# Attention outputs in four 32-column strips instead of two 64-column halves, in a fused NSA and MLA layer

## The chip, the cores and the metric

One core of a Trainium2 chip runs the whole kernel as one program. The metric is the device time of one execution in microseconds (us), as the median of several runs. The profile is one execution taken by the hardware profiler.

## The reference, cut to what matters

The reference is one layer of a hybrid decoder: 512 prompt tokens and 8 decode tokens (each with 4096 cached positions) go through Native Sparse Attention (three branches: compressed, selected, sliding window) and Multi-head Latent Attention (MLA), each with 8 heads, then gates, projections, an output projection, a norm and a residual. All arrays are float32. For the prompt the part that matters here is the last product of attention, probabilities times values:

```python
o_s = jnp.einsum('bqgrkl,bqgkld->bqgrd', p_s.astype(v_sel.dtype), v_sel)      # selected branch
o_w = jnp.einsum('bqgrs,bsgd->bqgrd', p_w.astype(kvw.dtype), kvw[..., 1, :])  # sliding window
p = _masked_softmax(s, mask)                                                  # MLA
return jnp.einsum('bhqs,bsc->bqhc', p.astype(c.dtype), c)
```

Each is, for one head and one tile of 128 query tokens, a sum over blocks of 128 keys of (128 keys x 64 value columns), transposed, times (128 keys x 128 queries). The MLA values are expanded per head to 64 columns ahead of the stage (`vm`).

## The kernel before

The program is written engine by engine, with every order and every semaphore by hand; nothing is planned by a compiler. It has four stages: the input projection (to about 130 us), a preparation (to about 200 us), the attention stage (about 200 to 510 us), and the gates, projections and output (to the end).

**The attention stage** works on 96 *units*. A unit is one branch (selected, window or MLA), one head and one tile `tl` of 128 queries; it has `tl + 1` key blocks, 1 to 4. Two units with neighbouring heads are a *pair*; there are 48 pairs. TensorE (PE) runs a loop over steps d = 1 to 49. Its parts, in the order of a step, with the line of their matmuls:

- `scores(d)` (L1132): the scores of the two units of pair d, 64 or 96 rows of weights by 128 columns.
- `dec_transposes(d - 1)` (L1279), where a decode chunk was scored in the step ahead: transposes with 128 columns.
- `dec_scores` (L1210) or `latent_scores` (L1235, with L1239 at the end of every second one): decode scores. Both load weights of 128 rows and 32 columns, four at a time, into the four 32-column strips of the array (`32 * j:32 * j + 32` in the bank). Ten steps have the first, 32 the second (two of these are ahead of the first call of `outputs`: d = 0 and 1).
- `outputs(d - 2)` (L1153): the probabilities of pair d - 2 times values; this is what the change touches. It is called in 48 steps.
- `latent_outputs` (L1250, 128x32 weights, 256 moving columns; twice in each of 16 steps) or `dec_outputs` (L1219, 128x32 weights; in 10 steps), where a decode chunk is due.
- `gate_half` (L1266, 128x128 weights, 260 moving columns), in 16 steps.
- `dec_keys` (L1200) and `transposes` (L1140): 128-column transposes of cached keys and of the probabilities of pair d - 1.

In `outputs(p)` the values are the weights (stationary), the transposed probabilities `PTb[e]` are moving, and both heads of the pair (e = 0, 1) write their half of the partitions of bank 3. Ahead of it PE waits for `pt_by_V` and `pt_by_A`: VectorE (DVE, L2148) and ScalarE (ACT, L1678) copy the transposed probabilities out of PSUM. Behind it, `o_ps` releases DVE, which reads the bank (L2172, L2174), and the two copies.

The softmax of the units runs on DVE (L2140, mask and sum; L1782 and L1783, scaling) and ACT (L1670, exponential). Decode chunks take a chain of their own over DVE (L2192 to L2238), ACT (L1684, L1687, L1484) and back to PE.

**Loads.** SyncE (SP) issues the cached latents (`latents`, L619 to L622), windows (`windows`, L609) and weights in one queue, each behind a wait for a free slot, which PE frees with `mv_ps` or `do_ps`. GpSimd (POOL) gathers rotary keys and selected rows (L710).

A float32 matmul is carried out as two instruction pairs, each a weight load (PEld) and a matmul (PE); the profile counts these.

Of the kernel before, what the change touches and what calls it, by code (L numbers as in the profile page):

```python
# [16 lines left out]
P = 128  # L17
# [146 lines left out]
def build(nc, t):  # L164

    ctx = ExitStack()
    with ctx:
# [35 lines left out]
        bank = [ctx.enter_context(nc.psum_tensor(f"bank{i}", [P, 512], F32)) for i in range(8)]  # L203
# [65 lines left out]
        PTb = [c_(512) for _ in range(2)]  # L269
# [254 lines left out]
        def qbank(i):  # L524
            return bank[(3, 0, 4, 1)[i % 4]]
# [27 lines left out]
        def unit(u):  # L553

            if u < 32:
                return 2, 2 * (u // 8) + u % 2, (u % 8) // 2
            v = u - 32
            return (v % 4) // 2, 2 * (v // 16) + v % 2, (v % 16) // 4
# [4 lines left out]
        def group_of(p):  # L563

            return (p, True, True) if p < 16 else (16 + (p - 16) // 2, p % 2 == 0, p % 2 == 1)

        def pt_by(u):
            return "A" if u % 2 else "V"
# [240 lines left out]
        def _(pe):  # L809
# [156 lines left out]
            for b in range(4):  # L966
                for e in range(2):
                    n = 4 * e + b
                    mm = pe.matmul(bank[5][32 * e:32 * e + 32, 0:P], QZraw[:, n * 64 + 32 * e:n * 64 + 32 * e + 32], KcT[:, n * P:(n + 1) * P],
                                   start=(b == 0), stop=(b == 3))  # L970
# [16 lines left out]
            for n in range(10, 16):  # L987
                c, w = GROUPS[n]
                mm = pe.transpose(bank[7][0:w, P + 8 * n:P + 8 * n + 8], projD[0:DEC, c:c + w], ident8)
# [9 lines left out]
            for k in range(4):  # L999
                mm = pe.matmul(bank[2][32 * k:32 * k + 32, :], kcBD[:, (k // 2) * 32:(k // 2 + 1) * 32], qTraw[:, k * 512:(k + 1) * 512],  # L1000
                               start=True, stop=True)
# [4 lines left out]
            for i, h in enumerate(HQ):  # L1006
# [10 lines left out]
                for j in range(3):  # L1017
                    mm = pe.matmul(qbank(i)[:, :], wq[:, j * 1024 + h * P:j * 1024 + (h + 1) * P],  # L1018
                                   qdnT[:, j * TOK:j * TOK + SEQ], start=(j == 0), stop=(j == 2))
                mm.then_inc(S["qm_ps"], 1)  # L1020
                if i == 1:
                    pe.wait_ge(S["prep_by_act"], BY_ACT["sct"])
                    for tl in range(TILES):
                        mm = pe.transpose(bank[2][:, tl * P:(tl + 1) * P], pcP[:, tl * P:(tl + 1) * P], ident)
# [5 lines left out]
                if i == 4:  # L1030
# [3 lines left out]
                    for j in range(3):  # L1034
                        for s in range(4):
                            mm = pe.matmul(bank[6][32 * s:32 * s + DEC, 0:256], qdnT[:, j * TOK + SEQ:(j + 1) * TOK],
                                           wq[:, j * 1024 + s * 256:j * 1024 + (s + 1) * 256], start=(j == 0), stop=(j == 2))
                    mm.then_inc(S["prep_ps"], 1)
                if i == 6:
                    pe.wait_ge(S["prep_by_act"], BY_ACT["qd8"])  # L1040
                    for h2 in range(8):
                        mm = pe.transpose(bank[6][:, 256 + 8 * h2:264 + 8 * h2], qd8[0:DEC, h2 * P:(h2 + 1) * P], ident8)
# [3 lines left out]
            for p2 in range(4):  # L1046
# [3 lines left out]
                for ck in range(2):  # L1050
                    mm = pe.matmul(bank[KM_BANK[p2]][:, :], wk[:, ck * 512 + p2 * P:ck * 512 + (p2 + 1) * P],
                                   cT[:, ck * TOK:ck * TOK + SEQ], start=(ck == 0), stop=(ck == 1))
# [3 lines left out]
            for b in range(4):  # L1056
                for e in range(2):
                    n = 4 * e + b
                    mm = pe.matmul(bank[5][32 * e:32 * e + 32, 384:512], PcZ[:, n * 64 + 32 * e:n * 64 + 32 * e + 32], VcD[:, n * P:(n + 1) * P],
                                   start=(b == 0), stop=(b == 3))  # L1060
# [5 lines left out]
            for half in range(2):  # L1066
                for j in range(4):
                    h = 4 * half + j
                    c = h * 8 - 24 * half
                    mm = pe.matmul(bank[7][32 * j:32 * j + 32, half * 256:(half + 1) * 256], qmd[0:64, c:c + 32],  # L1070
                                   wkT[0:64, h * 256:(h + 1) * 256], start=True, stop=True)
            mm.then_inc(S["absorbed"], 1)

            for tl in range(TILES):
                if tl == 2:
                    pe.wait_ge(S["qmd"], 3)
                    for blk in range(4):
                        mm = pe.transpose(bank[6][:, blk * P:(blk + 1) * P], Pd[:, blk * P:(blk + 1) * P], ident)
# [6 lines left out]
                for ck in range(2):  # L1085
                    mm = pe.matmul(bank[VM_BANK[tl]][:, :], cT[:, ck * TOK + tl * P:ck * TOK + (tl + 1) * P],
                                   wv[:, ck * 512:(ck + 1) * 512], start=(ck == 0), stop=(ck == 1))
# [4 lines left out]
            for tl in range(TILES):  # L1092
                mm = pe.transpose(bank[4][:, tl * P:(tl + 1) * P], pcP[:, tl * P:(tl + 1) * P], ident)
# [14 lines left out]
            def values(br, tl, kb, h):  # L1108
                if br < 2:
                    at = kb * 256 + br * P + (h // 4) * 64  # L1110
                    return VV[:, at:at + 64]
                return vm[:, kb * 512 + h * 64:kb * 512 + (h + 1) * 64]
# [30 lines left out]
            def outputs(p):  # L1143

                g, first, last = group_of(p)
                for u in (2 * p, 2 * p + 1):
                    pe.wait_ge(S["pt_by_" + pt_by(u)], u // 2 + 1)
                if first and g:
                    pe.wait_ge(S["o"], g)
                br, h, tl = unit(2 * p)  # L1150
                for kb in range(tl + 1):
                    for e in range(2):
                        mm = pe.matmul(bank[3][64 * e:64 * e + 64, 0:P], values(br, tl, kb, h + e), PTb[e][:, kb * P:(kb + 1) * P],  # L1153
                                       start=(first and kb == 0), stop=(last and kb == tl))
                mm.then_inc(S["o_ps"], 1)

# [131 lines left out]
            for d in range(1, PAIRS + 2):  # L1288
# [8 lines left out]
                if d >= 2:  # L1297
                    outputs(d - 2)
# [83 lines left out]
            def quad(bk, k, rhs, first, last):  # L1382

                for j in range(4):
                    mm = pe.matmul(bk[32 * j:32 * j + DEC, 0:P].rearrange("p (r c) -> p r c", r=2), h_[k][:, SEQ:TOK],
                                   rhs.rearrange("p (r j c) -> p r j c", r=2, j=4)[:, :, j], start=first, stop=last)
                return mm
# [40 lines left out]
            for v, (kind, x) in enumerate(tail):  # L1428
# [20 lines left out]
                for hf in range(2):  # L1449
                    bk = bank[2 * (v % 2) + hf]  # L1450
                    bank_free(pe, v, 2 * (v % 2) + hf)
                    if kind in ("ga", "gb", "ma", "mb"):
                        for k in range(KM):
                            at = k * 256 + (x % 2) * P
                            mm = pe.matmul(bk[:, 0:HALF], gate_w[g % 2][:, at:at + P], X2[:, k * TOK + hf * HALF:k * TOK + (hf + 1) * HALF],  # L1455
                                           start=(k == 0), stop=(k == KM - 1))
                    else:
                        for k in range(KM):
# [3 lines left out]
                            if x < TILES:  # L1462
                                mm = pe.matmul(bk[:, :], h_[k][:, x * P:(x + 1) * P], w, start=(k == 0), stop=(k == KM - 1))  # L1463
                            else:
                                mm = quad(bk, k, w, k == 0, k == KM - 1)
# [1178 lines left out]
```

## Time and profile before

| | us |
|---|---|
| runs of the kernel before (3) | 743.08, 744.10, 747.31 |
| median | 744.1 |
| span of the profiled execution | 739.6 |
| PE busy in it | 692.4 (94%), 5305 matmul instructions |
| DVE busy | 440.6 (60%) |
| ACT busy | 211.5 (29%) |
| POOL busy | 123.4 (17%) |

The span runs from the first to the last instruction of the profiled execution; the time of a run includes what lies around it. The engines run beside each other, and a busy share says nothing of what waits for what; the chain of work followed back from the last instruction does. In the lines of the profile L12 is line 12 of the kernel, PE the matmuls, PEld the weight loads, "issue" a time for which nothing that the profile shows was waited for. Matmuls are pipelined and their ends are modelled, so neighbouring groups overlap in the rows; starts are measured.

### The profile page before, as it was taken

Reading aid. Unit: us, or ns where it says so; the run is one execution under the profiler, and the core shown is the slowest. Engines: PE = TensorE matmul, PEld = TensorE weight load, DVE = VectorE, ACT = ScalarE, POOL = GpSimd, SP = SyncE. Lnnn points to the kernel's source line nnn. Section 1 sums busy time; section 2 is a strip of 40 time slices with the busy share of each in tenths; the row PEclk is TensorE's granted clock in tenths of the full one; section 3 lists DMA queues with packets and bytes.
Section 4 is the critical chain, followed back from the end, with each engine's and each line's share of the span. In section 5 each row is a group of like instructions: output and inputs, shape, how many; then the busy total and the mean of one; then the engine's idle time right before and its main releaser. Section 6 shows DMA issues by size and latency. Waiting matters only on the chain.

```text
span 739.6 us, 14391 instructions
## 1 busy us (share of the span) xinstructions
PE 692.4 (94%) x5305; PEld 443.7 (60%) x5305; DVE 440.6 (60%) x1233; ACT 211.5 (29%) x579; POOL 123.4 (17%) x130
## 2 busy tenths in 40 slices
PE   9997999999988979789999999899999999999996
PEld 4443444644555655467675676557778888885452
DVE  3297799478666756764654554542577565644244
ACT  0302215555334434433533442321110101110111
POOL 0343340113042230321412202320000000000000
PEclk9999999999999999999999999999999999999998
DMA  9999994951779999967755686996210303026011
GB/s 343 414 414 421 418 399 159 384 219 49 250 276 336 315 381 343 393 222 277 276 209 185 237 285 232 332 334 259 72 57 1 114 1 114 1 91 280 29 47 41
DMA packets 57367, 170.27 MB, mean 230 GB/s; under 512 B 7537, under 2 KB 7690, under 8 KB 50514
## 3 DMA queue, kind: packets, MB, share of 16 engines
q1 hardware_dynamic: 47352, 120.68, 45.1%
q0 software_dynamic: 9600, 48.38, 16.6%
q8 instruction: 43, 0.70, 0.4%
q10 hardware_dynamic: 346, 0.29, 0.1%
q14 instruction: 26, 0.21, 0.1%
HBM read 164.99 MB, written 8.52 MB: 235 GB/s over the span
## 4 chain that ended last, share of the span: by engine, by line
PE 75%; DMA 9%; DVE 5%; issue 5%; SPq 3%; ACT 2%; another core or an unknown queue 1%; DVEq 0%; ACTq 0%
PE bank L1423 18%; PE bank L855 7%; PE bank L1463 7%; PE bank L1266 7%; DMA W<-w_attn 4%; PE bank L1153 4%; PE bank L1132 3%; PE bank L1250 3%; PE bank L1235 3%; PE bank L1018 3%; PE bank L1140 3%; DMA projP<-x 2%; PE bank L1200 2%; PE bank L1455 2%; DMA ring<-latent 2%
## 5 line engine op out<-in xcount | busy, mean ns | idle before, releaser
L710 POOL DMA_INDIRECT KRR<-krT,idxi x64 | 61.2, 957 | 221.9 <-PE bank L1239 207.1
L855 PE MATMUL bank<-W,XG 128*128 128x494 f32 x192 | 85.2, 589 | 4.2 <-DMA W<-w_attn 3.7
L1484 ACT ACTIVATE projP<-bank 128x128 f32<-128x128 f32 (+5 forms) x87 | 33.9, 391 | 110.0 <-PE bank L1423 47.5
L2438 DVE TENSOR_TENSOR projP<-projP,bank 128x260 f32<-128x260 f32 x83 | 33.9, 422 | 45.1 <-PE bank L1423 44.4
L855 PEld LDWEIGHTS bank<-W,XG 128*128 128x128 f32 x192 | 35.8, 195 | 41.0 <-issue 39.8
L1266 PE MATMUL bank<-W 128*128 128x260 f32 x256 | 60.4, 389 | 0.0
L1484 ACT ACTIVATE W<-bank 128x512 f32<-128x512 f32 (+2 forms) x69 | 40.1, 582 | 69.8 <-PE bank L898 18.7
L1670 ACT ACTIVATE projP<-bank,projP 128x128 f32<-128x128 f32 (+3 forms) x96 | 49.7, 524 | 29.9 <-DVE projP L2140 29.5
L2140 DVE CUSTOM_DVE_ANT_0 bank<-bank,maskb 128x128 f32<-128x128 f32 (+3 forms) x96 | 45.8, 507 | 15.9 <-PE bank L1132 11.2
L1266 PEld LDWEIGHTS bank<-W 128*128 128x128 f32 x256 | 47.3, 190 | 10.4 <-issue 3.3
L1463 PE MATMUL bank<-ring,W 128*128 128x512 f32 x112 | 49.5, 594 | 1.3 <-issue 1.3
L710 POOL DMA_INDIRECT ring<-cmp,idxi x32 | 38.7, 1209 | 72.1 <-DVE VV L1849 52.5
L1132 PE MATMUL bank<-W 64*128 64x128 f32 (+7 forms) x192 | 46.2, 467 | 1.4 <-ACT projP L1670 1.0
L1849 DVE TENSOR_TENSOR VV<-ring 128x1024 f32<-128x1024 f32 x32 | 39.1, 1222 | 7.4 <-DMA ring<-cmp,idxi 5.0
L1140 PE MATMUL bank<-cst,projP 128*128 128x128 f32 x240 | 37.8, 287 | 2.4 <-issue 1.3
L1423 PE MATMUL bank<-ring 128*128 128x260 f32 x168 | 38.3, 383 | 0.7 <-DVE ring L2404 0.7
L1463 PEld LDWEIGHTS bank<-ring,W 128*128 128x128 f32 x112 | 21.1, 190 | 27.7 <-issue 27.5
L1423 PEld LDWEIGHTS bank<-ring 128*128 128x128 f32 x168 | 31.8, 190 | 6.3 <-issue 1.5
L1140 PEld LDWEIGHTS bank<-cst,projP 128*128 128x128 f32 x240 | 28.2, 145 | 11.9 <-issue 6.4
L1423 PE MATMUL bank<-W 128*128 128x260 f32 x144 | 34.7, 384 | 0.4 <-DVE projP L2434 0.4
L1235 PE MATMUL bank<-ring,projP 128*32 128x128 f32 x800 | 29.2, 276 | 5.1 <-issue 3.2
L1744 ACT ACTIVATE projP<-projP 128x260 f32<-128x260 f32 x28 | 11.4, 420 | 72.8 <-DVE projP L2438 72.8
(439 smaller groups left out, 1145.7 us busy)
## 6 DMA issues: line engine op xcount, KB each, us to landing
ring<-latent SPq DMA_DIRECT2D x200, 256.0 KB
XG<-latent SPq DMA_DIRECT2D x56, 256.0 KB
W<-w_gate SPq DMA_DIRECT2D x12, 1024.0 KB, 4.7
W<-w_attn SPq DMA_DIRECT2D x16, 494.0 KB, 9.8
ring<-w_out SPq DMA_DIRECT2D x2, 2048.0 KB
o_win<-win SPq DMA_DIRECT2D x1, 4088.0 KB
W<-xT SPq DMA_DIRECT2D x1, 2080.0 KB, 11.2
projP<-x SPq DMA_DIRECT2D x1, 2048.0 KB
```

The source lines that it names most:

```text
L710: pool.indirect_dma_start(out=dst, out_offset=None, in_=src, in_offset=bass.IndirectOffsetOnAxis(ap=idxi[:, col:col + 1], axis=0)).then_in ...
L855: mm = pe.matmul(bank[2 * (u % 2) + n][:, 0:GW], XG[:, k * TOK + tl * P:k * TOK + (tl + 1) * P], w_part(half, k, n), start=(k == 0), stop= ...
L1132: pe.matmul(bank[x % 2][:, 0:width], q, kk, start=True, stop=True).then_inc(S["s"], 1)
L1140: mm = pe.transpose(pt_bank(u)[:, kb * P:(kb + 1) * P], Pb[u % 4][:, kb * P:(kb + 1) * P], ident)
L1235: pe.matmul(bank[5][32 * j:32 * j + 32, 0:P], latent_q(b, ck, 2 * i2 + q2), page(m, j, q2, 256 + ck * P, 256 + (ck + 1) * P), start=(i2 == ...
L1266: mm = pe.matmul(bank[6][:, 0:HALF], gate_w[g % 2][:, at:at + P], X2[:, k * TOK + hf * HALF:k * TOK + (hf + 1) * HALF], start=(k == 0), st ...
L1423: mm = pe.matmul(pair_bank(v, name)[:, 0:HALF], stationary(a, kk), moving(b, kk), start=(kk == 0), stop=(kk == inner - 1))
L1463: mm = pe.matmul(bk[:, :], h_[k][:, x * P:(x + 1) * P], w, start=(k == 0), stop=(k == KM - 1))
L1484: return act.activation(dst, src, ACT.Copy, scale=scale)
L1670: act.activation(Pb[u % 4][:, 0:w], bank[u % 2][:, 0:w], ACT.Exp, bias=NMp[:, u:u + 1], scale=-1.0, accum_out=RSp[:, u:u + 1]).then_inc(S[ ...
L1849: dve.tensor_tensor(sum4, x[:, 0:1024], x[:, 1024:2048], ALU.add).then_inc(S["summed"], 1)
L2140: dve.tensor_tensor_reduce(bank[u % 2][:, 0:w], bank[u % 2][:, 0:w], maskb[:, 512 - w:512], -1.0, 1e38, ALU.add, ALU.min, NMp[:, u:u + 1]) ...
```

## The change

The block of `outputs` no longer does one matmul for each head with 64 weight columns, but two for each head with 32. The loop runs over four strips: strip 0 and 1 are the lower and upper 32 value columns of head e = 0, strip 2 and 3 those of e = 1. Each writes its 32 partitions of bank 3. Both strips of a head have the same moving operand. What is computed, the bank, the place of `outputs` in the step, the waits ahead of it and the semaphore behind it are as they were. No other line changes.

```diff
                 br, h, tl = unit(2 * p)
                 for kb in range(tl + 1):
-                    for e in range(2):
-                        mm = pe.matmul(bank[3][64 * e:64 * e + 64, 0:P], values(br, tl, kb, h + e), PTb[e][:, kb * P:(kb + 1) * P],
+                    for strip in range(4):
+                        e, lo = strip // 2, 32 * (strip % 2)
+                        mm = pe.matmul(bank[3][32 * strip:32 * strip + 32, 0:P], values(br, tl, kb, h + e)[:, lo:lo + 32], PTb[e][:, kb * P:(kb + 1) * P],
                                        start=(first and kb == 0), stop=(last and kb == tl))
                 mm.then_inc(S["o_ps"], 1)
```

## Rows read from the trace of the kernel before

**Rows 1.** The page's first part: busy us, share of the span, instructions.
```profile
PE 692.4 (94%) x5305; PEld 443.7 (60%) x5305; DVE 440.6 (60%) x1233; ACT 211.5 (29%) x579; POOL 123.4 (17%) x130
```

**Rows 2.** The page's fourth part: the chain that ended last, by engine and line.
```profile
PE 75%; DMA 9%; DVE 5%; issue 5%; SPq 3%; ACT 2%; another core or an unknown queue 1%; DVEq 0%; ACTq 0%
...
by line: PE bank L1423 17.6%; PE bank L855 7.5%; PE bank L1463 7.5%; PE bank L1266 7.0%; issue 4.6%; DMA W<-w_attn 4.1%; PE bank L1153 3.8%; PE bank L1132 3.5%; PE bank L1250 3.5%; PE bank L1235 3.4%; PE bank L1018 3.1%; PE bank L1140 2.7%;
```

**Rows 3.** Windows of the attention stage: stretch, length, busy, clock, DMA share, GB/s.
```profile
200.00:300.00 100.00, 88.17 (x1259) 58.36 (x1259) 65.61 (x247) 40.89 (x139) 26.72 (x28) 0.98 0.94 333
300.00:515.00 215.00, 197.30 (x2237) 136.62 (x2235) 112.92 (x395) 75.17 (x231) 45.79 (x48) 0.98 0.75 268
```

**Rows 4.** Groups of L1153 by form; then those that start before 300 us.
```profile
L1153 PE MATMUL bank<-projP,VV 128*64 128x128 f32 x320 | 25.5, 286 | 4.0 <-issue 2.1 <-DVE projP L2148 2.0
L1153 PE MATMUL bank<-projP,W 128*64 128x128 f32 x160 | 12.3, 282 | 1.3 <-DVE projP L2148 1.0 <-issue 0.3
...
L1153 PE MATMUL bank<-projP,VV x24: 272/273/323, 285.1 to 297.6; 128*64 128x128 f32 x24
```

**Rows 5.** Timeline of PE, in three steps: start us, us, line, shape, instructions.
```profile
382.70 1.08 PE L1235 MATMUL bank<-XG,projP 128*32 128x128 f32 x32
383.60 0.40 PE L1239 MATMUL bank<-KRR,OB 128*32 128x128 f32 x8
383.93 1.09 PE L1153 MATMUL bank<-projP,VV 128*64 128x128 f32 x16
384.95 1.53 PE L1200 MATMUL bank<-cst,ring 128*128 128x128 f32 x12
...
402.78 0.44 PE L1153 MATMUL bank<-projP,VV 128*64 128x128 f32 x4
403.15 0.65 PE L1219 MATMUL bank<-ring,W 128*32 128x64 f32 x32
403.74 3.77 PE L1266 MATMUL bank<-W 128*128 128x260 f32 x16
...
409.10 1.08 PE L1235 MATMUL bank<-ring,projP 128*32 128x128 f32 x32
410.11 0.44 PE L1153 MATMUL bank<-projP,VV 128*64 128x128 f32 x4
```

**Rows 6.** Timeline of PE at the start of the stage.
```profile
202.13 0.62 PE L1178 MATMUL bank<-projP,cst 8*32 8x128 f32 x16
202.67 1.13 PE L1132 MATMUL bank<-W 96*128 96x256 f32 x4
```

**Rows 7.** The chain of waits in order of time, around the first window load.
```profile
265.21 8.83 DMA ring<-win
```

**Rows 8.** Timeline of PE in a step with keys; in brackets the idle time ahead.
```profile
390.89 0.45 PE L1279 MATMUL bank<-cst,W 128*128 128x128 f32 x1 [1.52 <-ACT W L1484]
```

**Rows 9.** The five largest waits of PE, 200 to 515 us: total us, times, longest.
```profile
PE bank L1250 <- issue: 4.3, 5, 1.7
PE bank L1235 <- issue: 3.2, 6, 1.2
PE bank L1153 <- DVE projP L2148: 3.0, 4, 1.1
PE bank L1279 <- ACT W L1484: 2.9, 4, 1.5
PE bank L1153 <- issue: 2.4, 4, 1.2
```

**Rows 10.** Timeline of PE at a hitch.
```profile
464.88 0.43 PE L1153 MATMUL bank<-projP,VV 128*64 128x128 f32 x2
465.69 0.27 PE L1153 MATMUL bank<-projP,VV 128*64 128x128 f32 x1 [0.38 <-issue]
466.42 0.27 PE L1153 MATMUL bank<-projP,VV 128*64 128x128 f32 x1 [0.46 <-issue]
467.13 0.69 PE L1250 MATMUL bank<-ring,projP 128*32 128x256 f32 x8 [0.45 <-issue]
```

## Prediction

> **What bounds the kernel now.** I read the page's busy table first [rows 1]: TensorE (PE) is busy 94% of the 739.6 us span, the next engine (VectorE, DVE) 60%. A busy PE is not yet the bound, so the chain of work that ended last came second [rows 2]: 75% of it is PE, 9% DMA, 5% DVE. Third, the stages [rows 3]. The changed line, L1153, runs only in the attention stage (206 to 509 us). From 200 to 300 us PE is busy 88.2 of 100 us and the DMA engines 94%; from 300 to 515 us PE is busy 197.3 of 215 us and DMA 75%. The change can therefore be worth most where PE ends the chain, and less in the first 100 us, where the transfers are nearly full. L1153 is 3.8% of the chain [rows 2], 28.1 us, of its 25.5 + 12.3 = 37.8 us busy [rows 4]: 74% of this line's time lies on the path that sets the end.
>
> Fourth, what a group of small matmuls costs on PE, from the timeline of PE in single steps. The time from one group's start to the next group's start is what counts, as the ends are modelled. A float32 matmul is two instructions, so a block of L1153 (two heads, e = 0 and 1) is 4 instructions. L1153 with 4 instructions takes 0.37 us to the next group, with 16 it takes 1.02 us [rows 5]: (1.02 - 0.37) / 3 = 0.217 us a block, that is two rounds of 0.109 us in which both column halves run together, plus 0.37 - 0.22 = 0.15 us once. This fixed part is the thing at stake. L1235, four 32-column strips, takes 0.90 us for 32 instructions when another four-strip group follows (L1239), but 1.01 us when L1153 follows [rows 5]. So eight rounds of four strips cost 8 x 0.109 + 0.03, and changing the shape of the weight tile costs 0.11 us more, before the first matmul of the new shape.
>
> **The change part by part.** It replaces per block two matmuls with 64 weight columns by four with 32; data, bank, order, waits and the semaphore stay. No DMA moves, and no wait is added.
>
> *Rounds.* Before: two halves together, 0.109 us. After: four strips with the same 128 moving columns. L1235 has exactly this form (128 rows, 32 columns, 128 moving columns) and also runs 0.109 us a round. The 240 rounds therefore keep their price: 0. What is new is that two neighbouring strips read the same moving tile. L1178 does that too (four strips, one moving tile, though of 8 rows): its 16 instructions take 0.54 us to the next group, of another shape [rows 6], four rounds and one shape change. So sharing costs nothing there.
>
> *Shape changes in front of L1153.* Counted by the plan: 48 steps call outputs(). In 30 of them latent_scores() stands directly ahead (32 calls less the two ahead of the first outputs()), in 10 dec_scores(); both use 32-column strips. These 40 lose the change, 0.11 us each = 4.4 us. They also lose the slow first round: of the fixed 0.15 us of L1153 some 0.10 us is the change to the next shape, priced like the one ahead, and the rest, 0.05 us, a longer first round, which a group that continues a shape doesn't have: 40 x 0.05 = 2.0 us. In the other 8 a 128-column transpose stands ahead, and the change stays; the first round becomes as cheap as that of L1235 (0.03): 8 x 0.02 = 0.2 us.
>
> *Shape changes behind L1153.* In 26 steps a strip product follows (16 latent_outputs, L1250; 10 dec_outputs, L1219). They lose 0.10 us and their own slow first round, 0.02 us: 26 x 0.12 = 3.1 us. In the other 22 a 128-column group follows; a four-strip group is up to 0.03 us longer than its rounds (L1235 above), of which I take half: 22 x 0.015 = 0.3 us is lost.
>
> *PE alone:* 4.4 + 2.0 + 0.2 + 3.1 - 0.3 = **9.4 us**, if nothing else were ever late.
>
> *What of it reaches the end.* By the 74% of L1153 on the chain: 7.0 us. From 200 to 300 us stand 184 of the 480 instructions of L1153 [rows 3, 4], so about 2.6 us of the 7.0. There the window load that PE waits for (L1200) was issued at 265.21 us and took 8.83 us [rows 7]. It was issued when PE had freed the slot, which speaks for keeping the gain; but it landed behind full DMA engines (94%), which speaks against. I take half: -1.3 us. Later PE waits for others where its own gain lies between their start and the wait: for ScalarE's copy at L1484 1.52 us ahead of L1279 [rows 8]. The two largest sums of such waits are 3.0 us for DVE and 2.9 us for ACT, four waits each [rows 9]. A step's gain is about 9.4 / 48 = 0.2 us, so if each of the eight swallows the gain of one to two steps it is 1.6 to 3.1 us less, most of which the 74% has already left out: -0.7 us. Left: **5.0 us**. The profiled span would go from 739.6 to 734.6 us. The median of the runs, 744.1 us, lies 4.5 us above the span; the same distance gives **739.1 us**.
>
> *More instructions.* 240 matmuls more are 480 matmul and 480 weight-load instructions, on 1259 + 2237 = 3496 of each in the stage [rows 3], +14%. PE has times there in which it waits for nothing the profile shows: ahead of the strip groups and L1153 4.3 + 3.2 + 2.4 = 9.9 us in 15 pieces [rows 9]. Some are hitches in the midst of a group with no wait in it: at 464.88 us in L1153 itself, where four instructions needed 2.25 us instead of 0.37 [rows 10]. From below, a hitch is no matter of instruction count, or longer groups of one form even hide some, and this costs 0 or a little less; from above, the 9.9 us grow faster than the count. Nearest is the row of L1219 [rows 5], 32 instructions in 0.59 us, 18 ns each, with no hitch, denser than the 27 ns that the new L1153 needs. I take 0, and keep +1.4 us (14% of 9.9) for the range.
>
> A rule of the Trainium skill speaks against the change. "TensorE: Matmul & The Clock Gate", in Part 1 under "Wait — 56ns, not 53.3ns?", says that with hardware decoding off the sequencer needs about 62 ns per matmul and becomes the bound when the array's work per matmul is shorter. By it a four-strip round would take 4 x 62 = 248 ns, and 240 rounds some 33 us more. The trace disagrees: L1235 runs 32 matmul instructions in 0.90 us, 28 ns each [rows 5].
>
> **The rivals.**
> 1. *All of it arrives.* The load waits and the vector work move up with PE, because both start from semaphores that PE raises: 9.4 us, 734.7 us. For it: PE is 75% of the chain and the slot frees hang on it. Against: the DMA engines at 94% in the first part. 14%.
> 2. *The others set the pace.* The DMA-fed first part keeps its time, and in the rest the softmax and key copies of DVE and ACT do: what is left is under a quarter, 9.4 x 0.2 = 1.9 us, 742.2 us. For it: PE is already made to wait in the stage for 29.5 us altogether by its busy time (315 less 285.5) [rows 3]. Against: the longest wait for DVE or ACT is 1.5 us [rows 9], and its start hangs on PE's own earlier work. 24%.
> 3. *Slower: the instruction supply.* Doubling the instructions of L1153 makes PE run out of them more often; the place is the dense runs latent_scores, outputs, latent_outputs, in 200 to 300 and 445 to 500 us. It decides when the 9.9 us grow by half (5.0 us); if they double with the line's instructions: 744.1 - 5.0 + 9.9 = 749.0 us. For it: one hitch stands inside L1153 [rows 10]. Against: L1219. 14%.
> 4. *It doesn't do what it says:* the four strips don't run in one round, as two share a moving tile of 128 rows, or as the instructions don't pair up four at a time. Then each round takes two, 240 x 0.109 = 26.2 us more, less some of the 5.0: about 766 us. Against: L1235 and L1178. 3%.
>
> **How the numbers follow.** Forecast 45%, rivals 14, 24, 14 and 3%. The forecast's own spread is about 2 us to either side (half or none of the first part's gain; +1.4 us for instructions). The range from 735.0 to 746.0 us leaves out the lower half of rival 1, rival 4 and most of rival 3. About 0.5% (3.7 us) is what a measurement of this kernel can tell from no change: faster means under 740.4 us. That is rival 1 and about three quarters of the forecast, with a little of rival 2: 0.50. Slower means above 747.8 us, most of rival 3 and rival 4: 0.15. The rest, 0.35, is within.
>
> **What would show it.** In the profile after: L1153 as 960 matmul instructions of 128x32; 32 of L1235 followed by L1153 after 0.90 us instead of 1.01; L1153 with one block 0.22 us instead of 0.37 in front of L1219 or L1250, but still near 0.38 in front of L1140. If these hold and the span has moved by much less than 5 us, the step that failed is the share that reaches the end, and the waits of PE for DMA, DVE and ACT must have grown by the difference. If PE's idle time for nothing shown ahead of these groups has grown from 9.9 past 15 us, rival 3 holds. If a block takes 0.43 us and more, rival 4 does. The prediction would be wrong from the start if the 0.11 us turned out to belong to the 64-column form rather than to the change of form.

## The result and the profile after

The change made the kernel slower: 756.49 us as the median of 4 runs (752.26 to 758.16) against 744.68 us (743.08 to 747.31) for the kernel before beside it, a ratio of 1.0142 with a 95% interval of 1.0100 to 1.0183. (The recorded ratios are worked out from the single runs; the two medians alone give 1.0159.) The span of the profiled execution is 754.0 us. The forecast was 739.1 us: the sign was wrong. In the comparisons further down, the few runs over 1.5% above the fastest of their kernel are left out of medians and ratios.

First the page of the kernel after: busy us and share of the span with the number of instructions, then the chain that ended last. They answer to [rows 1, 2].

```profile
PE 693.0 (92%) x5785; PEld 451.4 (60%) x5785; DVE 440.5 (58%) x1233; ACT 211.1 (28%) x579; POOL 124.2 (16%) x130
...
PE 77%; DMA 5%; DVE 5%; another core or an unknown queue 4%; issue 4%; SPq 2%; ACT 1%; DVEq 0%; ACTq 0%
```

The 480 instructions more cost PE 0.6 us of busy time. But the chain has a part that was 1% [rows 2] and is now 4%, some 30 us: "another core or an unknown queue". There is only one core. It is time in which an engine waited for a semaphore (the counter by which one engine tells another that its work is done; to raise it is an *increment*) and the profile found nobody who raised it just then. In the rows of waits it is called "remote".

Second the same stretches of the attention stage as in [rows 3], in the kernel after: length, then busy us (instructions) of PE, PEld, DVE, ACT and POOL, granted clock of PE, DMA share, GB/s.

```profile
200.00:300.00 100.00, 82.27 (x1259) 54.19 (x1257) 60.28 (x228) 38.23 (x130) 24.75 (x26) 0.95 0.87 307
300.00:515.00 215.00, 188.87 (x2399) 134.82 (x2400) 112.30 (x396) 73.98 (x229) 47.91 (x51) 0.94 0.73 255
```

PE was idle for 29.5 us of these 315 before and is idle for 43.9 now. The DMA engines are less full than before (87% against 94%) and the granted clock is lower (0.95 and 0.94 against 0.98). PE is not busier; it waits more.

Third, who waits for that unnamed release, from 200 to 530 us: engine, what, line, then us in total, times, longest. First the three largest of the kernel before; I had not read them when I wrote the prediction:

```profile
ACT projP L1484 <- remote: 11.1, 6, 2.6
DVE bank L2140 <- remote: 4.0, 4, 1.4
DVE projP L2222 <- remote: 2.1, 1, 2.1
```

and of the kernel after (a line number of after is that of before plus one):

```profile
ACT projP L1485 <- remote: 26.0, 7, 5.2
ACT W L1485 <- remote: 13.6, 5, 4.8
DVE W L2205 <- remote: 12.2, 3, 5.1
DVE projP L2149 <- remote: 7.9, 3, 4.6
DVE OB L2173 <- remote: 7.9, 2, 4.7
DVE bank L2141 <- remote: 5.3, 4, 1.6
DVE projP L2223 <- remote: 2.2, 1, 2.2
```

With a fourth row of 0.9 us that makes about 18 us before, and 75 us after; the longest single wait grew from 2.6 to 5.2 us. All of these are instructions that copy or read a bank which PE has filled. One place in the timeline of the kernel after shows what happens (start us, us, engine, line; in brackets the idle time ahead and what ended it):

```profile
258.95 0.40 PE L1240 MATMUL bank<-KRR,OB 128*32 128x128 f32 x8
259.17 1.06 PE L1154 MATMUL bank<-projP,W 128*32 128x128 f32 x32
...
260.16 0.44 PE L1140 MATMUL bank<-cst,projP 128*128 128x128 f32 x2
260.43 1.45 PE L1132 MATMUL bank<-W 96*128 96x384 f32 x4
...
263.40 0.94 POOL L710 DMA_INDIRECT KRR<-krT,idxi  x1 [0.30 <-issue]
...
265.37 0.29 DVE L2173 COPY OB<-bank 128x128 f32<-128x128 f32 x1 [4.66 <-remote]
265.44 0.45 ACT L1485 ACTIVATE projP<-bank 128x128 f32<-128x128 f32 x2 [5.24 <-remote]
...
265.92 0.43 PE L1154 MATMUL bank<-projP,W 128*32 128x128 f32 x8 [3.92 <-DVE projP L2149]
```

DVE (L2173) waits for the outputs of L1154, which PE had finished at 260.23 us, and ACT (L1485) for transposes (L1140) that ended at 260.60 us. Both start only at 265.4 us. In between, from 259.65 us, POOL works on a group of four indirect gathers (L710), the last of which ends at 264.34 us. PE itself then starves for 3.92 us, and from 262 to 266 us it does nothing. In the windows of PE alone (busy, clock, DMA share, GB/s) the granted clock falls behind that idle time, from the upper level (2.4 GHz) to a mean of 0.57, which is mostly the lower one (1.2 GHz), and comes back:

```profile
262.00:266.00 4.00, 0.08 (x4) 1.00 1.03 368
266.00:270.00 4.00, 4.00 (x43) 0.57 0.85 275
270.00:274.00 4.00, 4.00 (x61) 1.00 0.95 378
```

The trace also has the time at which each increment was seen. PE's increments from matmuls that ended between 260.23 and 262.00 us were all seen only between 265.35 and 265.54 us. So PE's semaphore increments reach the others late, during the gathers. I counted them in the records of the traces from about 200 to 540 us: an increment is "late" when it is seen more than 0.3 us after its matmul's end. Before: 64 of 104 increments inside a gather group are late, 5 of 263 outside. After: 81 of 108, and 2 of 262. The increments are held for up to 5 us and then often arrive together. The counts are approximate: some increments have no time of their own in these traces and are left out.

### The profile page after: what moved, and what is told of

Same layout as the page of the kernel before. It is cut to its first block, busy times and chain, and to the rows that moved or that the text cites. A ratio compares the mean times of both kernels' runs of the same rounds, so it can differ in the third digit from the quotient of the medians.

```text
span 754.0 us, 15351 instructions
## 1 busy us (share of the span) xinstructions
PE 693.0 (92%) x5785; PEld 451.4 (60%) x5785; DVE 440.5 (58%) x1233; ACT 211.1 (28%) x579; POOL 124.2 (16%) x130
## 3 DMA queue, kind: packets, MB, share of 16 engines
q0 software_dynamic: 9600, 48.38, 16.2%
## 4 chain that ended last, share of the span: by engine, by line
PE 77%; DMA 5%; DVE 5%; another core or an unknown queue 4%; issue 4%; SPq 2%; ACT 1%; DVEq 0%; ACTq 0%
PE bank L1424 17%; PE bank L1267 7%; PE bank L1464 7%; PE bank L855 7%; PE bank L1251 4%; DMA W<-w_attn 4%; PE bank L1236 4%; PE bank L1132 4%; PE bank L840 3%; PE bank L1154 3%; PE bank L1018 3%; PE bank L1140 2%; PE bank L1456 2%; PE bank L1201 2%
## 5 line engine op out<-in xcount | busy, mean ns | idle before, releaser
L710 POOL DMA_INDIRECT KRR<-krT,idxi x64 | 62.0, 968 | 226.3 <-PE bank L1240 211.5
L1485 ACT ACTIVATE projP<-bank 128x128 f32<-128x128 f32 (+5 forms) x87 | 33.5, 391 | 118.6 <-PE bank L1424 47.5
L1485 ACT ACTIVATE W<-bank 128x512 f32<-128x512 f32 (+2 forms) x69 | 39.8, 581 | 77.9 <-PE bank L898 18.0
L710 POOL DMA_INDIRECT ring<-cmp,idxi x32 | 38.6, 1206 | 71.3 <-DVE VV L1850 52.2
L1140 PE MATMUL bank<-cst,projP 128*128 128x128 f32 x240 | 38.3, 288 | 12.2 <-DVE W L2205 12.2
L1132 PE MATMUL bank<-W 64*128 64x128 f32 (+7 forms) x192 | 47.8, 485 | 1.3 <-ACT projP L1671 0.8
L1140 PEld LDWEIGHTS bank<-cst,projP 128*128 128x128 f32 x240 | 28.0, 145 | 22.6 <-DVE W L2205 13.4
L1236 PE MATMUL bank<-ring,projP 128*32 128x128 f32 x800 | 29.7, 281 | 7.1 <-DMA ring<-latent 4.2
L1236 PEld LDWEIGHTS bank<-ring,projP 128*32 128x32 f32 x800 | 21.5, 111 | 19.6 <-issue 14.6
## 6 DMA issues: line engine op xcount, KB each, us to landing
W<-xT SPq DMA_DIRECT2D x1, 2080.0 KB, 11.8
```

The source lines that it names most:

```text
L710: pool.indirect_dma_start(out=dst, out_offset=None, in_=src, in_offset=bass.IndirectOffsetOnAxis(ap=idxi[:, col:col + 1], axis=0)).then_in ...
L1132: pe.matmul(bank[x % 2][:, 0:width], q, kk, start=True, stop=True).then_inc(S["s"], 1)
L1140: mm = pe.transpose(pt_bank(u)[:, kb * P:(kb + 1) * P], Pb[u % 4][:, kb * P:(kb + 1) * P], ident)
L1236: pe.matmul(bank[5][32 * j:32 * j + 32, 0:P], latent_q(b, ck, 2 * i2 + q2), page(m, j, q2, 256 + ck * P, 256 + (ck + 1) * P), start=(i2 == ...
L1485: return act.activation(dst, src, ACT.Copy, scale=scale)
```

## The experiments

My theory after this, called the gather theory in the expectations: **(A)** the shape changes are gained as forecast, but PE's increments are held while POOL works on a gather group, the more so the more PE instructions stand there. Rivals: **(B)**, the shape theory: the strip form itself is slower somewhere, in rounds or in sharing a moving tile; **(C)**, the count theory: the number of PE instructions costs by itself, gathers or not.

The kernels ran on several chips, each comparison on one chip with the kernel before beside it. The chips turned out to be of two kinds. On chips 13, 14 and 15 the kernel before takes about 722.7 us and increments are hardly ever late (I call them *punctual*). On chips 0 and 9 it takes 745 to 751 us, and in the traces taken there of versions with all gathers in their old place most increments inside gather groups are late (*late* chips; the traces of the first measurement show it as well). Only chip 0 was used twice, and it was late both times.

**First comparison, a punctual chip.** The key gathers taken away in all pairs but the first, in the kernel before and after. These kernels use the first pair's rotary keys for all pairs, so they leave out a part of the decode scores. Of the 19 gather groups of the stage 15 go; four groups that gather selected rows stay:

```diff
-                for j in range(4):
+                for j in range(4 if p2 == 0 else 0):
...
-                    pe.wait_ge(S["kr_landed"], 64 * (p2 + 1))
+                    pe.wait_ge(S["kr_landed"], 64)
```

> The kernel before, but GpSimd gathers the rotary key rows (KRR, 4 indirect gathers) only for the first of the 16 latent pairs; the other 15 pairs use the same rows, so this part of the decode scores is not computed. Gather theory: in the traces of both kernels the semaphore increments of TensorE arrive late (by 0.3 to 4.3 us) almost only while GpSimd works on a group of four indirect gathers, so without them the late increments and the idle times that hang on them go: 728 to 737 us against 744.7. Count theory (too many small instructions for TensorE's sequencer, wherever they stand): only the few us of transfers change, 742 to 745 us.

> The changed kernel with the same part left out: rotary key rows gathered for the first latent pair only. Gather theory: the loss of the change is its meeting with the gathers, so it turns into the gain worked out for TensorE alone, 5 to 9 us less than the kernel before with one gather. Count theory: the changed kernel stays 8 to 15 us slower than the kernel before with one gather. Shape theory (four strips that share a moving tile, or write 32 partitions each, are what is slow): the same, 8 to 15 us slower.

The instruction count doubled without the strip form (two halves of 64 columns stay, each block is cut in two along the queries):

```diff
-                    for e in range(2):
-                        mm = pe.matmul(bank[3][64 * e:64 * e + 64, 0:P], values(br, tl, kb, h + e), PTb[e][:, kb * P:(kb + 1) * P],
+                    for half in range(4):
+                        e, lo = half % 2, 64 * (half // 2)
+                        mm = pe.matmul(bank[3][64 * e:64 * e + 64, lo:lo + 64], values(br, tl, kb, h + e), PTb[e][:, kb * P + lo:kb * P + lo + 64],
```

> The kernel before with its 64-column halves, but each matmul of the outputs split into two of 64 moving columns: as many instructions as in the changed kernel (960 matmuls and 960 weight loads at this line), no change of shape saved or added, rounds half as long. Gather and count theory: the instruction count is what hurts, so it is slower than the kernel before by 8 to 22 us (the changed kernel's +12, and its shape gain missing). Shape theory: as before, within 3 us.

And strips only in the 17 steps in which neither the step nor the one ahead has a gather group, halves in the others:

```diff
+            def far_from_gathers(d):
+                return not any(M_at.get(x, 0) % 2 for x in (d - 1, d))
...
+                    strips = 4 if far_from_gathers(p + 2) else 2
```

> Four strips only in the 17 steps that are neither the step in which a group of gathers is released nor the one behind it; 64-column halves in the other 31. All of the computation. 16 of the 40 shape changes ahead and 10 of the 26 behind go: 16 x 0.16 + 10 x 0.12 = 3.8 us of TensorE. Gather theory: nothing is added in the groups of gathers, so it is 1.5 to 4 us faster than before: 741 to 743 us. Count and shape theory: a third of the change's loss, 3 to 5 us slower than before.

Measured: e1 720.81 us, e2 713.08, e3 721.10, e4 718.54, and the kernel before 722.50. So here taking the gathers away gives nothing clear of noise (0.9971, interval 0.9940 to 1.0003), and doubling the count costs nothing (0.9994, 0.9955 to 1.0032). e4 gains 4.0 us (0.9949). Without gathers the change gains 7.7 us (e2 against e1). For e1 both expectations missed. For e3 those of (A) and (C) missed and that of (B), within 3 us, came true; for e2 and e4 it was (A) that came true, and (B) and (C) missed. No theory fits all four, as they were made from a late chip. That left a new question: is it the kernel or the chip?

**Second comparison, a punctual chip.** The kernel after and before again, and both with the gathers moved. For the move the keys get two buffers (`KRR` and a free part of `projD`), and the release behind `ds` becomes one behind an output step:

```diff
-                if p2:
-                    pool.wait_ge(S["ds"], mla[p2 - 1]["q"] + 1)
+                    pool.wait_ge(S["mv_ps"], 2 * p2)
+                rows = krr(p2)
```

> The changed kernel, unchanged, once more beside the kernel before, since the kernel before took 744.7 us where the change was first timed and 722.5 us where the four variants were. Gather theory with a condition (the late increments appear in some places of measurement and not in others): if the kernel before comes out near 722 us, the changed kernel is 4 to 9 us faster than it; if near 744 us, it is 8 to 15 us slower. Count or shape theory without a condition: about 1.5% slower in either case.

> The kernel before, for its trace in this place. Gather theory: if its span is near 718 us, at most 3 semaphore increments of TensorE come over 0.3 us late in the groups of gathers; if near 740 us, 40 or more of about 100.

> The changed kernel, all of it computed, with the rotary key rows in two buffers and each group of gathers released by mv_ps, when the latent outputs of the pair ahead are done, no longer by ds, right ahead of the strip outputs. Gather theory: near 744 us for the kernel before, the groups meet fewer strips and more of gate_half, so it is 5 us or more faster than the changed kernel; near 722 us it is within 3 us of the changed kernel. Count or shape theory: within 3 us of the changed kernel in either case.

> The kernel before with the same move of the gathers, all of it computed. Gather theory: near 744 us for the kernel before, 3 to 10 us faster than it; near 722 us within 3 us. Count or shape theory: within 3 us in either case.

Measured: the kernel after (e5) 715.09 us, before 722.98: 0.9897 (0.9862 to 0.9932), **7.9 us faster**. It is the same program that is 11.8 us slower on the first chip. e5 at the same point of the program as above:

```profile
250.72 1.08 PE L1154 MATMUL bank<-projP,W 128*32 128x128 f32 x32
...
251.22 0.94 POOL L710 DMA_INDIRECT KRR<-krT,idxi  x1 [6.82 <-PE bank L1240]
251.73 0.44 PE L1140 MATMUL bank<-cst,projP 128*128 128x128 f32 x2
...
252.20 0.27 DVE L2173 COPY OB<-bank 128x128 f32<-128x128 f32 x1
252.21 0.28 ACT L1485 ACTIVATE projP<-bank 128x128 f32<-128x128 f32 x1 [0.43 <-PE bank L1140]
...
253.50 0.43 PE L1154 MATMUL bank<-projP,W 128*32 128x128 f32 x8
```

The gathers run at the same place with the same length (0.94 us each), the next L1154 comes 2.78 us after the last one instead of 6.75, and no wait of e5 or e6 in the stage is for an unnamed release (0 of 140 and 2 of 139 increments late inside gather groups). At this place PE's increments were seen within about 0.1 us of their matmuls' ends. So the increments are held only on some chips.

e7 and e8 took 774.09 and 782.31 us (1.0713 and 1.0837): I had released the gathers too late, and PE waited for the keys. PE's largest waits in e7:

```profile
PE bank L1240 <- DMA projP<-krT,idxi: 30.5, 5, 9.3
PE bank L1240 <- DMA KRR<-krT,idxi: 25.3, 5, 8.4
```

My expectations (within 3 us) missed by over 50 us, and the pair says nothing of late increments. But it repeats the gain: with the gathers moved in both, the kernel with strips (e7) is 8.2 us faster than the one with halves (e8).

**Third comparison, a late chip.** The same move released one pair earlier, beside the kernel after:

```diff
+                if p2 > 1:
+                    pool.wait_ge(S["mv_ps"], 2 * (p2 - 1))
```

> The changed kernel, unchanged, in a third place. By the gather theory the sign follows the place: near 722 us for the kernel before it is 6 to 9 us faster, near 744 us 8 to 15 us slower, and its trace has under 3 or over 60 late increments in the groups of gathers. Count or shape theory without such a condition: slower wherever it is measured, which the second place has already gone against.

> The changed kernel, all of it computed, with two buffers for the rotary key rows, each group of gathers released when the latent outputs of the pair two ahead are done. The former try released them when those of the pair ahead were done, and TensorE waited 30.5 + 25.3 us for their landing. Now they land a pair earlier, and this wait goes: within 3 us of the changed kernel where increments are not late; where they are, 3 us or more faster than it, since the groups no longer start right ahead of the strips.

> The kernel before with the same release, all of it computed. Where increments are not late: within 3 us of the kernel before. Where they are: 3 us or more faster than it.

Measured: e11 755.38 us against 745.20, 1.0142 (1.0075 to 1.0209), the first result over again. e9 took 752.87 and e10 755.52. Fewer increments are late (22 of 68 in e9, 35 of 77 in e10), yet e9 is only 2.5 us faster than e11, within the intervals, and e10 is 10.3 us slower than the kernel before, where I had expected 3 us or more of gain for each. (A) doesn't say why e10 loses. PE's largest waits in e9 are new ones, for nothing shown, ahead of `dec_outputs` (L1224) and `outputs` (L1158):

```profile
PE bank L1224 <- issue: 11.3, 17, 1.2
PE bank L1158 <- issue: 8.5, 13, 1.1
```

e10, with halves, has them too (11.1 and 3.9 us), so they come with the move and not with the strips; what they wait for stays open. Moving the gathers is no cure. One thing speaks for the gathers' part in it: with all 480 instructions more, e9 is 2.7 us faster than e10 (not clear of noise), where on the same chip e11 is 10.2 us slower than the kernel before.

**Fourth comparison, a late chip.** The three kernels of the first comparison that decide, where the increments are late:

> The kernel before with the rotary key rows gathered for the first latent pair only; that part of the decode scores is left out for the other 15 pairs. If this place is one with late increments (kernel before near 745 us): gather theory 716 to 726 us, the same as in a place without them; if lateness belongs to the place alone and not to the gathers, 740 to 746 us. In a place without them (near 722 us) 718 to 723 us by either.

> The changed kernel with the same part left out. Place with late increments: gather theory 709 to 719 us, 6 to 9 us less than the kernel before with one gather; if the extra instructions hurt there without gathers too, 5 us or more above it. Place without: 711 to 715 us.

> The kernel before with 64-column halves and each matmul of the outputs split into two of 64 moving columns: the instruction count of the changed kernel, its shapes those of before. Place with late increments: if the number of instructions issued beside the gathers is what makes them late, 15 to 25 us slower than the kernel before (the changed kernel's 10, and its 8 us of saved shape changes missing); if it is the four-strip form, within 3 us of it. Place without: within 3 us, as it was.

| kernel | us | against before, 751.26 | increments late inside groups |
|---|---|---|---|
| e12, before, without the 15 key groups | 722.25 | 0.9594 (0.9524 to 0.9664) | 6 of 13 |
| e13, after, without the 15 key groups | 709.42 | 0.9442 (0.9365 to 0.9518) | 6 of 15 |
| e14, count doubled, halves | 767.47 | 1.0208 (1.0140 to 1.0277) | 82 of 105 |

Without the key gathers the kernel before gains 29.0 us here, where on the punctual chip it gained 1.7. The same work and the same traffic went away on both, so they alone don't explain the gain; what also went here are the late increments (no wait for an unnamed release is left in e12 or e13). In windows, e12 has PE busy for 91.42 and 205.51 us at clock 1.00 and 0.99, where the kernel before had 88.17 and 197.30 at 0.98 in the first measurement [rows 3]:

```profile
200.00:300.00 100.00, 91.42 (x1309) 60.36 (x1309) 71.16 (x265) 44.76 (x148) 4.04 (x4) 1.00 0.97 352
300.00:515.00 215.00, 205.51 (x2295) 146.31 (x2295) 119.08 (x414) 74.15 (x230) 11.24 (x12) 0.99 0.70 250
```

And without the key gathers the change gains 12.8 us (e13 against e12). (B) falls, as strips that were slower by themselves would lose here too. So does (C): e13 has all 480 instructions more and loses nothing by them. e14 doubles the count at this line, keeps the old form, and loses 16.2 us, while the same kernel lost nothing on the punctual chip (e3). Its waits are those of the kernel after:

```profile
ACT projP L1485 <- remote: 28.8, 8, 5.3
ACT W L1485 <- remote: 15.8, 6, 4.9
DVE W L2205 <- remote: 13.8, 3, 5.1
DVE projP L2149 <- remote: 13.3, 6, 4.7
```

In these runs the count costs only where gathers and a late chip come together: of the three theories (A) is left. Two things were not run: e14's doubled count without gathers, and the full change on this chip with them. Each added matmul also brings a weight load, and no run tells the two apart.

**A version for both kinds of chip.** Strips only where no gather group stands, once in the 17 steps of e4, once in 28 steps (a gather group in the step ahead forbids strips only for d < 16):

```diff
-                return not any(M_at.get(x, 0) % 2 for x in (d - 1, d))
+                return not any(M_at.get(x, 0) % 2 for x in ((d - 1, d) if d < 16 else (d,)))
```

Punctual chip:

> Four strips only in the 17 steps that are neither the one in which a group of gathers is released nor the next, all of it computed. In a place without late increments it was 0.5% faster than the kernel before. In a place with them, gather theory: the added instructions stand away from the gathers, so the gain of 2 to 4 us stays; if more instructions anywhere hurt there, it is slower by 3 us or more.

> Four strips also in the 11 steps behind a released group from step 16 on, where the group (4.7 us) ends before the outputs of the next step; 28 steps in all, all of it computed. 25 x 0.16 + 21 x 0.12 = 6.5 us of TensorE. In either kind of place 3 to 6.5 us faster than the kernel before; in a place with late increments at least 10 us faster than the changed kernel's distance to the kernel before.

Late chip:

> The 28 steps outside the groups of gathers, as before, for another place. With late increments (kernel before near 745 us or over): gather theory 2 to 6.5 us faster than it; if more instructions anywhere hurt there, 5 us or more slower. Without: 3 to 6.5 us faster, as it was.

> The 17 steps away from the gathers, for another place. With late increments: gather theory 1 to 4 us faster than the kernel before; if more instructions anywhere hurt there, 3 us or more slower. Without: 2 to 4 us faster, as it was.

| strips in | punctual chip (before 722.79) | late chip (before 749.36) |
|---|---|---|
| 17 steps (e15, e18) | 719.18, 0.9946 (0.9920 to 0.9971) | 747.00, 0.9969 (0.9936 to 1.0003) |
| 28 steps (e16, e17) | 717.90, 0.9929 (0.9902 to 0.9956) | 745.74, 0.9944 (0.9910 to 0.9977) |
| all 48 steps (e5, e11; on two other chips) | 0.9897 (0.9862 to 0.9932) | 1.0142 (1.0075 to 1.0209) |

The 28-step version is faster than the kernel before on both kinds, by 4.9 and 3.6 us. The 17-step version is so on the punctual chip; on the late one its 2.4 us are within the interval, but it doesn't lose. So more instructions away from the gathers don't hurt on a late chip. On a punctual chip the full change has the better median (7.9 us), though the intervals overlap.

## Why the prediction was wrong, point by point

**TensorE's own gain: right.** L1154 in front of a transpose, in the timeline of the kernel after:

```profile
360.28 0.40 PE L1240 MATMUL bank<-KRR,OB 128*32 128x128 f32 x8
360.50 0.62 PE L1154 MATMUL bank<-projP,VV 128*32 128x128 f32 x16
361.05 1.21 PE L1201 MATMUL bank<-cst,ring 128*128 128x128 f32 x9
...
414.86 1.07 PE L1211 MATMUL bank<-W,projP 128*32 128x512 f32 x8
415.75 0.40 PE L1154 MATMUL bank<-projP,VV 128*32 128x128 f32 x8
```

L1240's 8 instructions take 0.22 us to L1154 (two rounds, no change of form), where the old L1239 took 0.33 us to L1153 [rows 5]. L1154 x16 takes 0.55 us to the 128-column group, four rounds and one change. Over all steps, the gap from the last start of the group ahead to the first start of the outputs fell from 202 to 89 ns behind L1235 and from 522 to 409 ns behind L1210, and from the outputs to L1219 or L1250 from 203 to 89 ns: 0.113 us each, the 0.11 of the sum. Within L1153, the time from the first start to the last fell by 0.037 us in each of the 48 steps (from 822 to 785 ns with four blocks, e6 against e5); the prediction had put 0.05 us on 40 steps and 0.02 us on the rest. In front of the 128-column groups nothing was lost (203 ns in both). The whole is 40 x 0.113 + 26 x 0.114 + 48 x 0.037 = 9.3 us, against the 9.4 of the prediction; its small errors cancel. The Trainium skill, "TensorEngine Tiling (Array Packing)", Key Properties, says that changing the tiling mode drains TensorE; it gives no price. The trace agrees that a change costs time, and its price here is 0.113 us.

**Rounds and the shared moving tile: right**, 0.109 us a round; rival 4 is out.

**What reaches the end: not refuted.** Where nothing is late, the change (e5) brings 7.9 us of the 9.4 against the kernel before beside it. The interval of 4.9 to 10.0 us holds the 5.0 us of the forecast at its edge and the 9.4 us of rival 1, and leaves out the 1.9 us of rival 2. The one pair of traces of that chip (e5 and e6, spans 714.1 and 719.8 us) gives 5.7 us. In it L1154 starts the stage 1.3 us later than L1153 did (206.81 against 205.51 us), is 0.2 us ahead at 298 us and 4.1 us ahead at its last call (483.85 against 487.97 us). That is 1.5 us gained by 300 us, where I had taken 1.3, and 3.9 us after it, where I had taken 3.7. Two traces can't settle such a split. The DMA engines are full up to 300 us in e5 (first row below: 365 GB/s at a share of 1.00), and PE's wait for the window load is as long as ever, 2.9 us in e6 and 3.1 us in e5 (second row):

```profile
200.00:300.00 100.00, 90.10 (x1506) 62.16 (x1506) 71.44 (x266) 45.11 (x149) 30.93 (x32) 0.98 1.00 365
...
PE bank L1201 <- DMA ring<-win: 3.1, 1, 3.1
```

**"More instructions": this step failed.** I took 0 and at most +1.4 us, from the times in which PE itself waits. On a late chip it costs 16.2 us (e14 on chip 0, 10.5 to 20.8 by its interval), which is more than the whole gain. Rival 3 named the count as well, with 749.0 us, but in the wrong place: it priced PE's own waits for nothing shown (9.9 us [rows 9]), and these did not grow (L1154 4.8, L1236 2.8, L1251 1.2 us, 8.8 in all). Its sign was right for a reason that it didn't have. What grew are the waits of DVE and ACT for PE's increments (18 to 75 us), and PE's waits for their results. PE's five largest waits of the kernel after, against [rows 9]:

```profile
PE bank L1140 <- DVE W L2205: 12.2, 5, 4.1
PE bank L1154 <- DVE projP L2149: 9.9, 5, 4.1
PE bank L1154 <- issue: 4.8, 4, 2.0
PE bank L1236 <- DMA ring<-latent: 4.2, 3, 2.6
PE bank L1280 <- ACT W L1485: 3.1, 3, 2.0
```

A warning stood in the trace of before, though not that more instructions would make it worse. The part "unknown queue" stood at 1% in the chain [rows 2], and I passed over it as noise. And the 1.52 us of [rows 8], which I priced as ScalarE's copy being slow, is such an increment. In the kernel before:

```profile
388.07 1.00 POOL L710 DMA_INDIRECT KRR<-krT,idxi  x1 [0.30 <-issue]
388.35 0.60 PE L1200 MATMUL bank<-cst,ring 128*128 128x128 f32 x4
...
390.04 0.60 ACT L1484 ACTIVATE W<-bank 128x512 f32<-128x512 f32 x1 [1.62 <-PE bank L1200]
```

PE ended at 388.95 us, ACT was free, and started 1.09 us later; the last gather ended at 389.07. The profile even names L1200 as the releaser. The trace has PE's increment at 390.01 us, 1.06 us after its matmul's end.

**The sum on a late chip.** -12.8 us without the key gathers (e13 against e12) and +16.2 us for the count (e14) give +3.4 us, and with the 7.9 us of the punctual chip +8.3; on the other two late chips 10.2 and 11.8 were measured. Each of the terms is uncertain by 3 to 5 us, so this neither contradicts the account nor leaves room for a proof that it is complete. A part of the rest can be the clock, 0.94 to 0.95 in the stage instead of 0.98; it falls behind idle time as shown at 266 us, so I take it for a consequence, which no run shows by itself.

## What to carry to other kernels

Putting neighbouring matmul groups into one form of weight tile was worth 0.11 us of TensorE's time here for each change of form that went; count the changes, and add nothing for rounds that stay the same. Before adding instructions to a full engine, look at the others' waits on it: where a copy starts a microsecond or more after the matmul that feeds it has ended, or a wait on one core is put down to "remote", the signals are what the others wait for, and more instructions there can cost more than the engine gains, as they did here. Put such a change in the steps that have none of these waits, and measure on more than one chip.

## What the runs showed of the hardware

- On some chips TensorE's semaphore increments arrive up to 5 us late while GpSimd works on a group of indirect gathers (4.7 us for four): 64 to 85 of about 105 increments inside the groups against 0 to 2 of 140 on the others. The kernel before takes 22 to 29 us more on these chips; on chip 0, 29.0 us go when 15 of the 19 gather groups go, and 1.7 us on a punctual one. Outside the groups increments are punctual everywhere (at most 9 of 261 late).
- More TensorE instructions make the loss larger: 480 more matmul instructions (each with its weight load), without a change of form, cost 16.2 us on such a chip and nothing on another (-1.4 us, within its interval).
- What distinguishes the chips, and what in a gather holds the increments back (GpSimd's own work, the descriptors it writes, or the path of the semaphores), was not tried and stays open. So does why more TensorE instructions make it worse; that they share some queue with the increments is only a guess.
